# The softmax's blocks in a hybrid attention and gated-MLP layer: turned by VectorE and a copy through DRAM instead of by TensorE

## The reference

```python
proj = h @ w_in[l]                    # h = rms_norm(x); 1024 x 7424 results
o_a  = sliding_window_attention(q, k, v, sinks, rel_bias)   # 16 query heads, 2 key/value heads, head size 64, window 128
y_a  = (o_a * silu(gate_a)) @ w_branch_a
o_b  = spatial_gating(gelu(u_b), gelu(v_b), ...)
y_b  = (o_b * silu(gate_b)) @ w_branch_b
out  = (sigmoid(mg_a) * y_a + sigmoid(mg_b) * y_b) @ w_out
x    = x + rms_norm(out)
```

```python
scores = q @ k.T * HEAD_DIM ** -0.5 + bias      # masked to the last 128 keys
m      = maximum(max(scores), sink)
p      = exp(scores - m)
probs  = p / (sum(p) + exp(sink - m))
out    = probs @ v
```

## Time and profile before

| | |
|---|---|
| runs | 909.92, 911.77, 911.94 us; median 911.77 |
| profiled execution | 907.86 us, its span 906.1 us |
| busy share of the span | TensorE 99%, VectorE 71%, ScalarE 54%, GpSimd 55% |
| chain that ended last | TensorE 98% |
| granted TensorE clock, mean | 0.998 |

### The profile page before, as it was taken

The page is one execution under the profiler, slowest core; times in us unless marked ns, Lnnn a source line. Parts: engine busy times, 40 slices in busy tenths (PEclk is TensorE's granted clock), DMA queues, the critical chain, the costliest instruction groups (busy, mean ns, idle before and its releaser), DMA issues.

```text
span 906.1 us, 12649 instructions
## 1 busy us (share of the span) xinstructions
PE 898.7 (99%) x4332; PEld 754.0 (83%) x4332; DVE 640.1 (71%) x1135; ACT 491.0 (54%) x948; POOL 499.4 (55%) x395
## 2 busy tenths in 40 slices
PE   9999999999999999999999999999999999999997
PEld 7888888888888888888888888888888888888886
DVE  6766794655656564656565678688689878989968
ACT  6554355766756675757566664344444434534563
POOL 4565235777686868695868685445542252043236
PEclk9999999999999999999999999999999999999999
DMA  8889764422222253323222243533188550435004
GB/s 307 195 200 247 243 204 106 136 77 90 71 91 85 82 139 129 94 77 98 72 84 91 82 150 95 187 122 122 59 303 323 186 209 1 139 116 210 1 1 186
DMA packets 126591, 122.50 MB, mean 135 GB/s; under 512 B 23208, under 2 KB 95936, under 8 KB 126272
## 3 DMA queue, kind: packets, MB, share of 16 engines
q1 hardware_dynamic: 124288, 118.27, 41.2%
q10 hardware_dynamic: 2240, 3.43, 1.2%
HBM read 89.68 MB, written 35.15 MB: 138 GB/s over the span
## 4 chain that ended last, share of the span: by engine, by line
PE 98%; ACT 0%; DVE 0%; POOL 0%; issue 0%; DVEq 0%; POOLq 0%; ACTq 0%
PE acc L970 51%; PE acc L1150 11%; PE acc L823 9%; PE ps_m L1150 7%; PE ps_t L1150 7%; PE ps_t L987 3%; PE ps_m L1017 3%; PE acc L913 2%; PE ps_t L997 2%; PE ps_t L853 1%; PE ps_m L853 0%; PE acc L1042 0%; PE ps_t L839 0%; PE ps_t L855 0%; PE ps_m L855 0%
## 5 line engine op out<-in xcount | busy, mean ns | idle before, releaser
L970 PE MATMUL acc<-mv,w_hi 128*128 128x512 f32 x1344 | 353.1, 392 | 0.0
L970 PEld LDWEIGHTS acc<-mv,w_hi 128*128 128x128 f32 x1344 | 245.0, 188 | 45.0
L970 PE MATMUL acc<-mv,w_lo 128*128 128x512 f32 x672 | 181.1, 391 | 0.0
L970 PEld LDWEIGHTS acc<-mv,w_lo 128*128 128x128 f32 x672 | 126.2, 188 | 28.3
L1751 POOL TENSOR_TENSOR w_lo<-sums,w_hi 128x1024 fp32r<-128x1024 f32 x48 | 116.0, 2418 | 46.4 <-ACT w_hi L1316 38.4
L1751 POOL TENSOR_TENSOR w_lo<-raw,w_hi 128x1024 fp32r<-128x1024 f32 (+1 forms) x48 | 95.7, 1994 | 41.5 <-ACT w_hi L1309 35.9
L1150 PE MATMUL acc<-right,left 128*128 128x512 f32 x432 | 98.7, 389 | 0.0
L1150 PEld LDWEIGHTS acc<-right,left 128*128 128x128 f32 x432 | 81.0, 188 | 17.2 <-DVE left L2131 0.4
L1796 POOL TENSOR_SCALAR_AFFINE_SELECT pt_prev<-pt_pack 128x512 fp32r<-128x512 f32 x64 | 41.7, 652 | 85.7 <-DVE pt_pack L2067 85.7
L1518 ACT ACTIVATE prob<-neg_s,neg_max 128x129 f32<-128x129 f32 x128 | 50.6, 397 | 68.6 <-DVE neg_max L2076 68.5
L823 PE MATMUL acc<-mv 128*128 128x512 f32 x288 | 69.3, 394 | 0.6 <-ACT mv L1183 0.6
(11 more groups left out here) (282 smaller groups left out, 1680.8 us busy)
## 6 DMA issues: line engine op xcount, KB each, us to landing
raw<-in_w_in SPq DMA_DIRECT2D x56, 512.0 KB, 4.0
ht_d<-sums SPq DMA_DIRECT2D x8, 512.0 KB, 5.1
mix_d<-mix_b SPq DMA_DIRECT2D x8, 512.0 KB, 3.9
ga_d<-gate SPq DMA_DIRECT2D x16, 256.0 KB, 2.0
tb<-tb_d SPq DMA_DIRECT2D x4, 1024.0 KB, 5.2
ub<-mix_d SPq DMA_DIRECT2D x7, 512.0 KB, 3.5
gb_d<-ub SPq DMA_DIRECT2D x7, 512.0 KB, 2.6
x_both<-in_x SPq DMA_DIRECT2D x6, 512.0 KB, 6.3
```

The lines of the kernel that those rows point to most:

```text
L970: ins = nc.tensor.matmul(bank, (w_lo if y == 2 else w_hi)[:, left + k * P:left + (k + 1) * P], right[:, (OPW if y == 1 else 0) + k * HALF: ...
```

## The change

TensorE no longer turns the blocks. Instead VectorE turns each 128x128 block of `prob` in place with its transpose instruction, which turns every 32x32 square of it where it stands (L2081 of the changed kernel). For two blocks at once, SyncE then writes `prob` to a new DRAM tensor `prob_d` and reads it back into `turned_in` by four transfers in pieces of 32 floats, which puts the squares in their places. The unpack reads `turned_in` in SBUF rather than PSUM, in step b+4 instead of b+3; the select moves to b+4, and the products with the values from b+5 to b+6. So the last results of a head pair fall into steps 14 and 15, which are steps 0 and 1 of the next one; `attention_all` gives both, the older one first. `prob` becomes a ring of two buffers of two blocks each, and the scores are written straight into it (`neg_s` goes, and the sink is now copied by VectorE for each block). `o_tmp` becomes one buffer. The weights are loaded one step later. Some semaphores are merged, which changes no wait of this part.

```diff
-                prob = [sb(f"prob{b}", [P, 2 * SINK_W], f32, s1) for b in range(3)]
-                o_tmp = [sb(f"o_tmp{b}", [P, 256], f32, s1) for b in range(2)]
+                prob = [sb(f"prob{b}", [P, 4 * SINK_W], f32, s1) for b in range(2)]
+                o_tmp = sb("o_tmp", [P, 256], f32, s1)
+                turned_in = sb("turned_in", [P, 512], f32, s1)
...
-        def neg_w(blk, h):
-
-            c = (blk % 2 * 2 + h) * SINK_W
-            return neg_s[:, c:c + SINK_W]
+        def prob_w(s, h, width):
+
+            c = (s % 2 * 2 + h) * SINK_W
+            return prob[s // 2 % 2][:, c:c + width]
...
+        def attention_all(n, s):
+
+            at = attention_at(n, s)
+            last = [(HEAD_PAIRS - 1, s + 14)] if n == FIRST_U + 1 and s < 2 else []
+            if at and at[0] and at[1] < 2:
+                last = [(at[0] - 1, at[1] + 14)]
+            return last + ([at] if at else [])
...
+            def prob_away(j):
+
+                sp.wait_ge(turn_ok, 2 * j + 2)
+                sp.dma_start(prob_d[j, :, :].rearrange("p (c j) -> p c j", c=4),
+                             prob[j % 2][:, :].rearrange("p (c j) -> p c j", c=4)[:, :, 0:P]).then_inc(prob_out[j % 2], 16)
+
+            def prob_back(j):
+
+                sp.wait_ge(prob_out[j % 2], 16 * (j // 2 + 1))
+                if j:
+                    sp.wait_ge(ptl_ok, 2 * j)
+                for g in range(4):
+                    sp.dma_start(turned_in[32 * g:32 * (g + 1), :].rearrange("a (c q b) -> a c q b", c=4, q=4),
+                                 prob_d[j, :, :].rearrange("(q a) (c g b) -> g a c q b", q=4, c=4, g=4)[g]
+                                 ).then_inc(prob_in[j % 2], 16)
+
             def attend(p, k):
+                if k in (2, 4, 6, 8):
+                    prob_away(4 * p + k // 2 - 1)
+                if k in (3, 5, 7, 9):
+                    prob_back(4 * p + k // 2 - 1)
...
-                    if s == 4:
+                    if s == (5 if n < FIRST_U else 4):
                         load_pair(n + 2, 0)
-                    if s == 5:
+                    if s == (6 if n < FIRST_U else 5):
                         load_pair(n + 2, 1)
...
-                if 5 <= k < 13:
-                    values(p, k - 5)
-                if 3 <= k < 11:
-                    transpose_p(p, k - 3)
+                if 6 <= k < 14:
+                    values(p, k - 6)
                 if k < 8:
...
-                if s >= 3:
-                    act.wait_ge(pt_done, s - 2)
                 for h in range(2):
-                    ins = nc.scalar.activation(prob[blk % 3][:, h * SINK_W:(h + 1) * SINK_W], neg_w(blk, h), ACT.Exp, scale=-1.0,
-                                               bias=neg_max[:, head(blk, h)], accum_out=row_sum[:, head(blk, h)])
+                    w = prob_w(s, h, SINK_W)
+                    ins = nc.scalar.activation(w, w, ACT.Exp, scale=-1.0, bias=neg_max[:, head(blk, h)],
+                                               accum_out=row_sum[:, head(blk, h)])
                 ins.then_inc(exp_ok, 1)
...
-                if k >= 7 and k % 2:
-                    g = (k - 7) // 2
+                if k in (8, 10, 12, 14):
+                    g = (k - 8) // 2
                     gg = 4 * p + g
                     act.wait_ge(values_ok, 2 * gg + 2)
-                    if gg >= 2:
-                        act.wait_ge(og_ok, gg - 1)
+                    if gg:
+                        act.wait_ge(og_ok, gg)
...
-                if 3 <= k < 11:
-                    blk = k - 3
+                if 4 <= k < 12:
+                    blk = k - 4
                     pool.wait_ge(ptl_ok, 8 * p + blk + 1)
                     if 8 * p + blk >= 2:
...
-                if k in (8, 10, 12, 13):
-                    g = (k - 7) // 2
+                if k in (9, 11, 13, 15):
+                    g = (k - 9) // 2
...
+                s = 8 * p + k
                 if k == 0:
                     if p == 0:
                         dve.wait_ge(made, MADE_BEFORE)
                     dve.wait_ge(bias_in, 16 * (p + 1))
                 if 1 <= k < 9:
                     m2 = slice((k - 1) % 4 * 2, (k - 1) % 4 * 2 + 2)
-                    dve.wait_ge(exp_ok, 8 * p + k)
+                    dve.wait_ge(exp_ok, s)
                     nc.vector.reciprocal(inv_den[:, m2], row_sum[:, m2]).then_inc(inv_ok, 1)
-                if 3 <= k < 11:
-                    s = 8 * p + k - 3
-                    dve.wait_ge(pt_done, s + 1)
-                    if s == 0:
-                        dve.wait_ge(v_out, 16)
-                    if s >= 2:
-                        dve.wait_ge(values_ok, s - 1)
-                    pack = pt_pack[(k - 3) % 2]
-                    own.link(nc.vector.tensor_copy(pack[:, 0:256], ps_p))
-                    nc.vector.tensor_tensor(pack[:, 256:512], ps_p, pack[:, 0:256].bitcast(f32), ALU.subtract).then_inc(ptl_ok, 1)
                 if k < 8:
-                    dve.wait_ge(scores_ok, 8 * p + k + 1)
-                    if 8 * p + k >= 2:
-                        dve.wait_ge(exp_ok, 8 * p + k - 1)
+                    if s % 2 == 0 and s >= 4:
+                        dve.wait_ge(prob_out[s // 2 % 2], 16 * (s // 4))
+                    nc.vector.tensor_copy(prob[s // 2 % 2][:, :].rearrange("p (b h j) -> p b h j", b=2, h=2)[:, s % 2, :, P],
+                                          sink_b[:, 2 * p:2 * p + 2])
+                    dve.wait_ge(scores_ok, s + 1)
                     if k > 0:
                         own.link(nc.vector.copy_predicated(blocks(ps_s)[:, :, 1, :], before_i, blocks(ps_s)[:, :, 0, :]))
                     for h in range(2):
                         bias = h * 256 + (0 if k else P)
                         ins = nc.vector.tensor_tensor_reduce(
-                            out=neg_w(k, h)[:, 0:P], in0=ps_s[:, h * 256 + P:(h + 1) * 256], in1=bias_t[:, bias:bias + P],
+                            out=prob_w(s, h, P), in0=ps_s[:, h * 256 + P:(h + 1) * 256], in1=bias_t[:, bias:bias + P],
                             scale=-HEAD_DIM ** -0.5, scalar=sink_b[:, 2 * p + h:2 * p + h + 1], op0=ALU.add, op1=ALU.min,
                             accum_out=neg_max[:, head(k, h)])
                     ins.then_inc(scores_used, 1)
-                if k >= 7 and k % 2:
-                    g = (k - 7) // 2
+                if 1 <= k < 9:
+                    dve.wait_ge(prob_ok, s)
+                    for h in range(2):
+                        w = prob_w(s - 1, h, P)
+                        ins = nc.vector.transpose(w, w)
+                    ins.then_inc(turn_ok, 1)
+                if 4 <= k < 12:
+                    e = s - 4
+                    dve.wait_ge(prob_in[e // 2 % 2], 64 * (e // 4 + 1))
+                    if e == 0:
+                        dve.wait_ge(v_out, 16)
+                    if e >= 2:
+                        dve.wait_ge(values_ok, e - 1)
+                    turned = turned_in[:, e % 2 * 256:(e % 2 + 1) * 256]
+                    pack = pt_pack[e % 2]
+                    own.link(nc.vector.tensor_copy(pack[:, 0:256], turned))
+                    nc.vector.tensor_tensor(pack[:, 256:512], turned, pack[:, 0:256].bitcast(f32),
+                                            ALU.subtract).then_inc(ptl_ok, 1)
+                if k in (8, 10, 12, 14):
```

More of the change, by code:

```diff
@@ L36 @@
 ACT_H, ACT_WSH = (1, 3), 2
+POOL_FRONT = 5
 Q_COL = 0
@@ L1805, in attend @@
                     pool.wait_ge(oadd_ok, 4 * p + g + 1)
[L1806 removed]
+                    nc.gpsimd.tensor_tensor(gate[p % 2][:, cols], o_tmp[:, :], gate[p % 2][:, cols], ALU.mult).then_inc(og_ok, 1)
             def left_sums_1(n):
```

100 lines of the change are left out of this document (38 added, 62 removed).

## The result

The changed kernel takes **966.79 us** (966.23 to 968.05, 4 runs), against 911.86 (909.92 to 912.35, 4 runs) for the kernel before in the same job: ratio 1.0623, 95% interval [1.060, 1.0647]. I had forecast 922 and a range up to 946: the sign was right and the size was not, +55 us in place of +10.

What follows compares the result with a forecast made beforehand. TensorE, busy 99% of the span, was taken to bound the kernel. Eight head pairs going from 47.44 to 48.78 us add 10.7 us to 907.9, giving 918.6; with 3.9 for the median of runs, 922 us; range 902 to 946.

Steps and rivals of the forecast that it cites:

- What goes: On TensorE: two turns a block, 0.22 us, go from 64 blocks, 14.1 us in all; nothing else changes there.
- Beside other work: VectorE's turns and sink copy add 0.5 us a step, hidden in idle time; later weights' loads taken at nothing.
- at nothing: Weights' loads issued behind the softmax transfers on SyncE's queue: no cost, or some tenths a pair if wrong.
- The port and the path: Block 5's unpack waits at the VectorE-GpSimd port until `w_lo` ends; GpSimd's order makes block 7's select 3.1 us late.
- the sum: Timeline of one head pair: 45.68 us if nothing waits, 48.78 with block 7's select 3.1 late, against 47.44 before.
- GpSimd's order: GpSimd runs a `w_lo` and sums ahead of block 7's select, so it, not the transfer alone, makes the last wait.
- The new loop: One-buffer `turned_in`: each read-back waits until the preceding pair is unpacked, so unpacks of blocks 2, 4 and 6 wait.
- The trip T: Transfer round trip from unpack to unpack: 0.1 + 3 x 0.45 + 2.35 = 3.8 us, between ends of 2.9 and 9.4.
- no gap: TensorE in steps 0 to 5 of a head pair: no gaps; some 3 us of them ahead of blocks 6 and 7.
- a sign of being wrong: Listed against the forecast: TensorE waiting for scores or a VectorE sum, or transfer issues of over 0.6 us each.
- A longer round trip: Rival: each of three trips hands on its excess; with T = 4.8, +35 us, 946; chance 0.17.

Runs made afterwards that it cites:

- the two kernels that have only the gain: The kernel before without TensorE's turns, 898.22 us; the changed kernel without the DRAM copy and with the unpack reading PSUM, 899.18 us.
- the transfers alone: Changed kernel with all transfers, but the unpack reads PSUM and waits for no read-back: 923.07 us; with raw loads issued first, 902.10 us.
- the unpack is from PSUM (899.18): Changed kernel without the copy to DRAM and back after the first two blocks, its unpack reading PSUM instead of SBUF: 899.18 us, ratio 0.9898.
- without a trip: Changed kernel without the copy to DRAM and back after the first two blocks, its unpack still reading SBUF: 914.56 us, ratio 1.0062.
- the sum first: Changed kernel with VectorE's additions into o_tmp issued before the unpack of the same step: 954.40 us, ratio 1.0503.
- half the transfers: Changed kernel with only two of the four read-back transfers for each two blocks after the first: 936.86 us, ratio 1.0317.
- the split issue: Changed kernel with two of each four read-back transfers issued by ScalarE's queue and two by SyncE's: 946.02 us, ratio 1.0403.
- the last kernel: "values later" with ScalarE copying turned blocks to PSUM, reordered, softmax write ahead of the second raw load: 901.74 us, 45.88 us a head pair.
- values later: "the kernel with 947.18" with everything from the unpack on one step later: 951.00 us, ratio 1.0462.
- the kernel with 947.18: Changed kernel with three softmax buffers, o_tmp sum before the unpack, sink copy late, and raw loads ahead of softmax transfers: 947.18 us.

## Why the prediction was wrong

- **What goes: right.** 14.1 us forecast; the two kernels that have only the gain show 1.2% and 1.0% (9 to 11 us), and the one of 45.88 us a head pair stands where the sum had 45.68.
- **Beside other work: mostly right.** Turns took 291 ns each where I had 0.2, hidden all the same. The sink copy, priced at 0.1, took 0.15 alone but 0.37 in the mean and up to 1.5, held at the port; I had asked only about operations with two SBUF inputs. The raw loads "at nothing" were wrong by themselves (22 us with the transfers alone); in the changed kernel `w_hi` waits only 8.1 us for them.
- **The port and the path: right.** Block 5's unpack waited for the end of that `w_lo`, 2.40 us, and block 7's select ends the head pair, as the sum had it. From the second head pair of the changed kernel, GpSimd and TensorE:

```profile
267.47 0.63 POOL L1800 TENSOR_SCALAR_AFFINE_SELECT pt_prev<-pt_pack 128x512 fp32r<-128x512 f32 x1
```

```profile
268.16 0.50 PE L1037 MATMUL ps_m<-pt_pack,v_st 128*128 128x256 f32 x2 [0.81 <-POOL pt_prev L1800]
```

  With no trip in it the sum has this select 2.1 late, at 44.5, and a head pair of 47.8; the trace has 44.7 and 48.1. But I put the loss on GpSimd's order, and that order costs nothing while the unpack is from PSUM (899.18).
- **The new loop: the step that failed.** The trip T was sized at 3.8 us, three times in a row. It is 4.8, 6.1 and 4.8. The 4.8 are issues of 0.65 where I had 0.45, three times, a landing of 2.6 for 2.35, and the hand-overs. The 6.1 are a case that I had left out: I let a trip begin at the unpack that frees `turned_in`, and never asked when the write had landed. That of blocks 4 and 5 stands behind a raw load, and its read-back starts 5.87 us after it. The sum with these three has block 7 selected at 45.5 + 1.0 + 2.3 + 1.0 = 49.8, 7.4 late, and gives 8 x (7.4 - 1.76) = 45 us more, 957; measured were 50.8 and 966.79.
- **What is left, 1 us a head pair.** The sum also began late: block 1 was unpacked 21.3 us after the head pair's start (401.77 less 380.46), not 18.8. It is so without a trip too. In the lines above, TensorE waits 0.80 us for VectorE's row maxima at block 1's scores, in a step where I had said no gap. That this makes the last 1 us is likely and was not run. TensorE's waits for the sum into `o_tmp`, which I had called a sign of being wrong, came, 29.4 us of them; but with the sum first, all but 11 us of the loss stayed, and these 11 are a block 5 unpacked earlier.
- **The rivals.** "A longer round trip" named the right mechanism, with 0.17, and T = 4.8 is right for two trips of three; its price, 946, lacked the late write. I had called issues of over 0.6 us a sign of being wrong, and they came.
- **Left open.** What the trip costs beyond the length shown for it: with half the transfers fewer bytes move too, and the split issue, with all the bytes and two issues in a row, stands 8 us above that. Whether ScalarE's waits alone make these 8 us was not separated. The write ahead of the load, worth 8 us in the last kernel, was not run on the changed kernel itself.

## What to carry to other kernels

When a wait is put into an in-order engine, find the one instruction on which each round of the loop ends (here block 7's select) and follow it through every experiment: it moved by what the time moved, while the waits listed for TensorE changed their names. Price all that the wait needs, the write as well as the read-back. A round trip through DRAM is write, issues and landing, some 8 us here from turn to data; it can be free if the buffers let it overlap and the step given to it is longer than it is. On a queue that works in order, its write belongs ahead of a bulk load, and its read-back, which waits, behind it: the first was worth 8 us, the second 22 with the transfers alone. When a fix gives nothing, read the waits again before dropping it: "values later" looked 4 us worse than what it was built on, and was the base of the fastest kernel once the port that had taken the trip's place was avoided. And look at more than one round: the head pair that I read first had the shortest middle trip of the eight.

## What was not expected of the hardware

- A copy of two elements a row from SBUF to SBUF waits for GpSimd as a whole block does: 141 ns at least, 2.23 us at 394.42 beside a `w_lo` of 2.55.
- The granted clock fell to its lower level behind a wait of 1.85 us (0.61 and 0.53 in the means of two stretches) and behind one of 2.28 (0.50), and was back within some 4 us. It stayed at 1.00 behind one of 1.61, but also behind one of 2.12 (471.07 in the changed kernel) and one of 2.33 (355.23 in the kernel with 947.18), so the length of the wait alone doesn't decide it.
- Four-dimensional transfers of 64 KB in rows of 32 floats take SyncE 0.64 us each to issue (median of 128; four took 2.61, or 3.54 at 425.61), against 0.34 for the gated results (256 KB) and 0.39 in the median for a raw load (512 KB). That it is their shape isn't shown: the merge gates' results (256 KB) took 0.49 to 0.63 in the median.
- A write of 256 KB issued 0.44 us behind a load of 512 KB had its read-back start 5.87 us after it; the median write landed after 2.8. The same shows on the merge gates' results: the eight that are issued next behind it (`ta_d<-c`) land after 5.6 in the median, the others after 2.7 to 3.5.
- VectorE's turns in place (267 to 316 ns, 128 times) never waited for GpSimd: two at 387.06 took 0.51 us together, beside a `w_lo` that ran from 386.51 to 388.91.
